# A sparse expert layer fetched in two steps: half rows, a mask, and tokens read from PSUM

## The reference, cut to what matters

```python
eidx = jnp.take_along_axis(cand_idx, pos, axis=-1)     # (token, head, 16)
g = jax.nn.softmax(best, axis=-1)
u = jnp.take(expert_u, eidx, axis=0)
h = jax.nn.gelu(jnp.einsum('thkd,td->thk', u, xb))
vv = jnp.take(expert_v, eidx, axis=0)
return jnp.einsum('thk,thkd->td', (g * h).astype(xb.dtype), vv)
```

## Time and profile before

| | before |
|---|---|
| median of 3 runs | 3214.2 us (3211.79 to 3214.63) |
| span of the profiled execution | 3210.9 us |
| PE, DVE, ACT, POOL busy, share of the span | 79%, 49%, 33%, 18% |
| DMA, mean | 333 GB/s |
| rows of the expert layer | from 1816 us to 3202 us |

### The profile page before, as it was taken

How to read it: one execution, slowest core, us unless ns; L and a number is a source line. 1 busy time by engine, 2 the same in 40 slices (tenths; PEclk the granted TensorE clock), 3 DMA queues, 4 the chain that set the end, 5 groups by cost and what they waited for, 6 DMA issues and landing times.

```text
span 3210.9 us, 43682 instructions
## 1 busy us (share of the span) xinstructions
PE 2530.9 (79%) x17242; PEld 1248.3 (39%) x17242; DVE 1564.1 (49%) x3391; ACT 1048.7 (33%) x2457; POOL 581.5 (18%) x535
## 2 busy tenths in 40 slices
PE   8999988797988878878879878897778655555655
PEld 6677774484322222222228634343324211111111
DVE  4655655763100100100107466678675777777764
ACT  2533443521000000000006354577344444343433
POOL 0000000000000000000000143344443444444442
PEclk9999998998999999999999989898888777788778
DMA  4211302249999999999995499999999999999997
GB/s 152 101 58 66 122 26 112 92 158 382 427 427 427 427 427 427 427 427 427 427 411 195 176 418 399 417 418 383 420 419 420 420 420 419 420 419 420 420 419 331
DMA packets 128670, 1067.80 MB, mean 333 GB/s; under 512 B 14289, under 2 KB 17233, under 8 KB 27601
## 3 DMA queue, kind: packets, MB, share of 16 engines
q0 software_dynamic: 75456, 543.20, 41.0%
q1 hardware_dynamic: 53008, 521.81, 39.4%
HBM read 1051.58 MB, written 13.37 MB: 332 GB/s over the span
## 4 chain that ended last, share of the span: by engine, by line
DMA 50%; PE 34%; DVE 7%; ACT 6%; issue 2%; POOL 1%; ACTq 0%; DVEq 0%; SPq 0%; POOLq 0%
PE ps L92 33%; DMA gb<-in_peer_uv,eidx 27%; DMA gw<-in_eu 14%; DMA gw<-in_ed 8%; DVE gb L146 2%; PE ps L97 2%; ACT L168 1%; ACT dots L168 1%; ACT diag L168 1%; ACT prob L168 1%; POOL gb L86 1%; DVE prob L146 0%; DVE w_lo L115 0%; ACT prob_t L168 0%; DVE prob L120 0%
## 5 line engine op out<-in xcount | busy, mean ns | idle before, releaser
L92 PE MATMUL ps<-gb,diag 64*64 64x512 f32 x4096 | 662.0, 759 | 410.3 <-ACT diag L168 396.8
L146 DVE CUSTOM_DVE_ANT_0 gb<-gb,xn 128x1024 f32<-128x1024 f32 x512 | 627.1, 1225 | 378.5 <-DMA gb<-in_peer_uv,eidx 378.0
L86 POOL DMA_INDIRECT gb<-in_peer_uv,eidx x512 | 570.3, 1114 | 1312.6 <-PE ps L92 718.5
L92 PEld LDWEIGHTS ps<-gb,diag 64*64 64x64 f32 x4096 | 148.2, 155 | 847.6 <-ACT diag L168 746.3
L168 ACT ACTIVATE dots<-dots 128x1 f32<-128x1 f32 (+1 forms) x382 | 77.6, 203 | 618.3 <-DVE dots L146 611.5
L115 DVE TENSOR_TENSOR expert_act<-expert_act,ps 128x512 f32<-128x512 f32 x32 | 22.0, 687 | 523.8 <-PE ps L92 523.2
L92 PE MATMUL ps<-ga,xt 128*64 128x512 f32 x1024 | 229.2, 596 | 41.3 <-DMA ga<-in_eu 32.6
L92 PE MATMUL ps<-gw,xt 128*64 128x512 f32 x992 | 224.3, 601 | 25.4 <-DMA gw<-in_eu 16.2
L168 ACT ACTIVATE diag<-cons,dots 128x128 f32<-128x128 f32 x512 | 205.5, 401 | 41.1 <-ACT dots L168 0.4
L115 DVE TENSOR_TENSOR x<-x,ps 128x512 f32<-128x512 f32 (+1 forms) x96 | 61.4, 643 | 296.5 <-PE ps L92 294.9
L168 ACT ACT_TABLE_LOAD x124 | 159.1, 1283 | 8.1 <-PEq L3241 0.7
(11 more groups left out here) (360 smaller groups left out, 3616.9 us busy)
## 6 DMA issues: line engine op xcount, KB each, us to landing
ga<-in_eu SPq DMA_DIRECT2D x47, 2048.0 KB, 35.5
gw<-in_eg SPq DMA_DIRECT2D x46, 2048.0 KB, 30.7
ring<-in_wt SPq DMA_DIRECT2D x75, 1024.0 KB, 6.0
gw<-in_ed SPq DMA_DIRECT2D x32, 2048.0 KB, 35.5
ga<-in_ed SPq DMA_DIRECT2D x32, 2048.0 KB, 36.1
ga<-in_eg SPq DMA_DIRECT2D x17, 2048.0 KB, 32.2
gw<-in_eu SPq DMA_DIRECT2D x16, 2048.0 KB, 35.5
p_scratch<-spill SPq DMA_DIRECT2D x35, 256.0 KB, 2.1
```

What stands on the lines that cost most here:

```text
L86: self.e.indirect_dma_start(out, None, table, bass.IndirectOffsetOnAxis(ap=idx, axis=0)).then_inc(s, 16)
L92: i = self.e.matmul(out, l, r, start=st, stop=sp, skip_group_check=True)
L146: self.done(self.e.tensor_tensor_reduce(out=o, in0=a, in1=b, scale=scale, scalar=start, op0=o0, op1=o1, accum_out=acc), name)
```

## The change

Rows 0 to 255 and 496 to 511 stay as they are. Of rows 256 to 495, each quad (four rows, n // 4) has one "whole" row, fetched as before (n % 4 == 0, but not rows 256 and 384), and three split ones. The table is seen as 32768 rows of 4 KB (`halves`), so index 2e is u and 2e + 1 is v. POOL fetches u of a split row; after the dots of the quad DVE makes the v indices and adds 65536 to those whose dot is at or below -11, which takes them past the end of the table, and POOL's second gather leaves these out. DVE also sets their weight to zero. 58 rows are whole and 182 are split; the v gathers of the first ten split rows (quads 64 to 66) fetch all, the other 172 are "gated". Of the 172 times 128 picks, 9610 fall at or below -11 by the same count as above (43.7%, 55.9 in a gather).

Four of the 13 buffers are kept for whole rows, nine are cut in a u and a v piece. A u piece is free after its dot, a v piece after its sum. The sums run one to two quads after the dots. The tokens of blocks 2 and 3 are written to PSUM (banks 0 to 3), and DVE's products read them there. The core of the diff:

```diff
+            self.e.indirect_dma_start(out, None, table, at, bounds_check=last, oob_is_err=False).then_inc(s, 16)
@@ second pass, its end @@
-        dv.wait_ge(("ffn_g", p))
+        dv.wait_ge(("ffn_g", p), ("f", p, 5))
         for i in (a, b_):
-            dv.tt(XN[i], XN[i], rowb, MUL, name=("xn3g", i))
+            dv.tt(XN[i] if i < 2 else XP[i - 2], XN[i], rowb, MUL, name=("xn3g", i))
@@ peer_order @@
+        g, j = n // 4, n % 4
+        before = [m for m in quad(g - 1) if whole(m)] if g > HALVED // 4 else []
+        later = [m for m in quad(g - 2) if not whole(m)] if g > HALVED // 4 + 1 else []
+        todo = later + before if g % 32 == 1 or g > WHOLE // 4 else before + later
+        return todo[j * len(todo) // 4:(j + 1) * len(todo) // 4]
@@ pe_peer @@
                 pe.wait_ge(("diag", n))
+                if not whole(n):
+                    pe.wait_ge(("v_row", n))
@@ ac_peer @@
+            elif ev[0] == "k":
+                ac.wait_ge(("mask", n // 4) if HALVED <= n < WHOLE else ("dot", n))
+                ac.act(d, d, ACT.Gelu_apprx_tanh, name=("gelu", n))
@@ dv_choose @@
         dv.stt(eidx[i % 2][:, 16 * h:16 * h + 16], e12[:, 0, :], 128.0, e12[:, 1, :], MUL, ADD, name=("eidx", i, h))
+        if i >= 2:
+            w_ = eidx[i % 2][:, 16 * h:16 * h + 16]
+            if (i, h) != (3, 7):
+                w_ = w_[:, 0 if h else 4:16:4]
+            dv.ts(w_, w_, 0.5, MUL, name=("eidx", i, h))
@@ dv_peer @@
-                dv.ttr(u, u, XN[i], 1.0, 0.0, MUL, ADD, dots[:, i % 2, k:k + 1], name=("dot", n), free=True)
+                dv.ttr(u, u, XN[i] if i < 2 else XP[i - 2], 1.0, 0.0, MUL, ADD, dots[:, i % 2, k:k + 1], name=("dot", n), free=True)
+            elif ev[0] == "k" and HALVED <= ev[1][0] < WHOLE:
+                if gated(n // 4):
+                    dv.ts(far, d, NO_GELU, ALU.is_le, FAR, MUL)
+                    dv.stt(e, far, 1.0, e, ADD, ADD, name=("v_idx", n // 4))
+                    dv.stt(s4, d, NO_GELU, s4, ALU.is_gt, MUL, name=("mask", n // 4))
+                else:
+                    dv.ts(e, e, 1.0, ADD, name=("v_idx", n // 4))
@@ po_peer @@
+        def v_row(n):
+            po.wait_ge(("v_idx", n // 4))
+            po.wait_ge(freed)
+            po.gather(v_of(n), halves, eidx[i % 2][:, k:k + 1], f"gv{s}", ("v_row", n), 2 * 16384 - 1 if gated(n // 4) else None)
+        for n in range(HALVED + 4):
+            u_row(n)
+        for g in range(HALVED // 4, WHOLE // 4):
+            for n in quad(g + 1):
+                u_row(n)
+            for n in quad(g):
+                if not whole(n):
+                    v_row(n)
+        for n in range(WHOLE + 4, 512):
+            u_row(n)
```

More of the change, by code:

```diff
@@ L2770, in block_program, with whole @@
     ROW_BUFFERS += [(t, GROW, ("used", 2 * TILES - 1)) for t in LATE]
[L2772 to L2777, removed]
-            held[s] = n
-        return slots
-    ROW_SLOTS = row_slots()
-    def row_group(n):
-        return (n,) if n < GROW or n >= LAST else (n, n + 1)
+    def whole(n):
+        return n < HALVED or n % 4 in (0,) and n % 128 != 0 or n >= WHOLE
@@ new lines, in quad, with places @@
+    def quad(g):
+        return range(4 * g, 4 * g + 4)
+    def places(rows, pieces, end, start=None):
+        held, out = list(start or [None] * len(pieces)), {}
+        for n in rows:
+            s = min((held[s] is not None, held[s] if held[s] is not None else s, s)
+                    for s, (_, first, _) in enumerate(pieces) if n >= first)[2]
+            freed = pieces[s][2] if held[s] is None else ("sum", held[s]) if held[s] < HALVED else (end, held[s])
+            out[n] = (s, freed, held[s] is None or held[s] < HALVED)
+            held[s] = n
+        return out, held
@@ new lines, in block_program @@
+    FIRST_AT, first_last = places(range(HALVED), ROW_BUFFERS, "sum")
+    KEEP = sorted(range(len(ROW_BUFFERS)), key=lambda s: first_last[s])[:4]
+    PAIRED = [s for s in range(len(ROW_BUFFERS)) if s not in KEEP]
+    KEPT = [(ROW_BUFFERS[s][0], 0, None) for s in KEEP]
+    U_PIECES = [(ROW_BUFFERS[s][0][:, 0:1024], 0, None) for s in PAIRED]
+    V_PIECES = [(ROW_BUFFERS[s][0][:, 1024:2048], 0, None) for s in PAIRED]
+    SPLIT = [n for n in range(512) if not whole(n)]
+    U_AT, u_last = places(SPLIT, U_PIECES, "dot", [first_last[s] for s in PAIRED])
@@ new lines, in u_of, with v_of, gated @@
+    def u_of(n):
+        return row_at(n)[0][:, 0:1024] if whole(n) else U_PIECES[U_AT[n][0]][0]
+    def v_of(n):
+        return row_at(n)[0][:, 1024:2048] if whole(n) else V_PIECES[V_AT[n][0]][0]
+    def gated(g):
+        return HALVED // 4 <= g < WHOLE // 4 and not any(V_AT[n][2] for n in quad(g) if not whole(n))
+    def row_group(n):
+        if n < GROW or n >= LAST:
+            return (n,)
+        if n < HALVED:
+            return (n - n % 2, n - n % 2 + 1)
+        return tuple(quad(n // 4))
@@ L2786, in peer_order @@
+    SUMS = [m for n in range(512) for m in sums_after(n)]
+    assert sorted(SUMS) == list(range(512)) and all(a // 128 <= b // 128 for a, b in zip(SUMS, SUMS[1:]))
+    SUM_AT = {m: q for q, m in enumerate(SUMS)}
+    ROW_ENDS = [SUMS[127], SUMS[255], SUMS[383], LAST - 1]
+    assert SUMS[LAST - 1] == LAST - 1
     def peer_order():
@@ L2791, in peer_order @@
         pass_rows = [24 + 31 * k // 10 for k in range(-1, 52)]
[L2792 to L2793 removed]
+        for n in range(512):
             group = row_group(n)
[L2795 to L2796 removed]
+            if n >= HALVED or n == group[0]:
+                ahead = 16 + min(8, n) + max(0, min(8, (n - 8) // 4))
+                need = min(32 * STEPS, STEPS * (ahead + (n if n >= HALVED else group[-1])) // 16) if n > 2 else STEPS
             while done < need:
@@ L2869, in pe_peer @@
             elif ev[0] == "w":
[L2870 to L2883, removed]
+                n = ev[1]
```

147 lines of the change are left out of this document (102 added, 45 removed).

## The result

The changed kernel took 3231.27 us (median of 4 runs, 3225.31 to 3232.83) beside 3213.64 for the kernel before (3211.79 to 3214.63): ratio 1.0052, 95% interval 1.0038 to 1.0066. It is slower by 0.5%, where 3152.6 us and a gain were forecast, and it lies outside the range. The same kernel measured in two other jobs gave 1.0087 (1.0066 to 1.0108), 3238.93 us in 4 runs, and 0.9913 (0.9884 to 0.9942), 3185.46 us in 2 runs. A job is a group of kernels that ran one after the other on one chip, with its own runs of the kernel before, which took 3213 to 3216 us in every one. Most of this document is about that difference between jobs.

What follows compares the result with a forecast made beforehand. DMA, full at 420 GB/s, was taken to bound the kernel before; after the change POOL, 533 us, plus 9 for waits and 5 for ends, 547 against 608.6, gives 3152.6 us; range 3120 to 3212.

Steps and rivals of the forecast that it cites:

- Sums one to two quads later hold v pieces longer, but nine pieces last three quads: Buffers for v halves: later sums cost nothing, as POOL asks for v(g) when sums of g - 3 are a quad old.
- the same matmuls: PE's work taken as unchanged, 1.46 us a row and 5.8 a quad, costed at nothing.
- POOL's work, 8.8 us a quad: POOL in the stretch: 422 gathers at 1.262 us a step, 533 us, 8.8 for a quad of seven.
- The bound check at zero: Comparing indices on gated gathers adds nothing on POOL; rival, chance 0.12: every tenth of a us adds 17.2 us.
- The new wait, 0.15 us a quad: POOL waiting for the v index before a quad's v gathers: 0.15 us on each of 60 quads, 9 us.
- the late-index rival: The two-quad index chain passes 17.6 us, POOL idles 0.6 us a quad: 3180 us, chance 0.18.
- the working: Index chain: v_idx(g) to the index two quads on takes 16.4 us, with 5.44 from gather start to product; slack 1.2.
- DMA: DMA in the stretch: 8.55 us a quad, 526 us in all; share 0.93 to 0.97, below POOL.
- Tokens in PSUM: Products reading PSUM stay at 1225 ns and no longer disturb POOL's gathers, taken at 0.96 us.
- The ends: Short queue at rows 496 to 511 and four whole rows costing more DMA: 5 us for both ends.
- picks not left out: Rival: an index past the end still moves data, DMA carries 624 us: 3235 us, slower, chance 0.03.

Runs made afterwards that it cites:

- e9: Kernel before with tokens of blocks 2 and 3 in PSUM and two gathers of 4 KB picks a row from row 256 on (u half twice): 3229.96 us.
- f2: The kernel before with tokens in PSUM and two 4 KB-pick gathers per row from row 256 on, repeated unchanged in another job: 3302.57 us.
- e8: Changed kernel with two rows in four split instead of three, six buffers for whole rows: 3174.78 us, ratio 0.9873.
- e5: Changed kernel with the tokens of blocks 2 and 3 back in SBUF: 3237.52 us.
- e6: Kernel before with only the tokens of blocks 2 and 3 in PSUM: 3213.68 us, ratio 1.0001.
- f4: Changed kernel a third time, unchanged, alone in another job (F): 3185.46 us, ratio 0.9913.
- e11: Changed kernel with two rows in four split and no pick left out: 3222.80 us, ratio 1.0026.
- e12: Changed kernel with one row in four split, picks left out as in the changed kernel: 3197.33 us, ratio 0.9946.
- e7: Kernel before with two gathers of 4 KB picks a row from row 256 on, both fetching the u half, tokens in SBUF: 3303.79 us.
- e1: Changed kernel with the limit at -1e30, so every gated gather fetches all 128 halves: 3228.86 us.
- e2: Changed kernel with the limit at 1e30, so every gated pick is left out: 3223.58 us.
- e10: Kernel before with each row from 256 on in two gathers of 64 picks of 8 KB (first 64 indices twice): 3480.78 us.

## Why the prediction was wrong, step by step

**The step that failed in the result.** "Sums one to two quads later hold v pieces longer, but nine pieces last three quads", and PE with "the same matmuls", both costed at nothing. That counts PE's matmuls, and not when their signals arrive; the cover it names for the v pieces is a quad, 8.8 us. Two waits hang on a sum: ACT's diagonal on the one four rows back, and POOL's v gather on the one three quads back. In late jobs signals came up to 14 us late, the circle of diagonal, matmul, signal, diagonal ran dry, and POOL waited for pieces. Beside that stands a second step, the wait for the index, set at 0.15 us a quad. In job A POOL stood idle for 65.5 us beyond the usual 0.305, in some 48.4 quads: 31 us for the index, 0.64 a quad, and 34 more for pieces, 0.71 a quad. 4 x 1.26 + 3 x 1.31 + 0.64 + 0.71 = 10.3 us a quad, against 10.15 before: the stretch is longer than before, where 547 us were forecast. Without the 0.71 it is 9.6, which is the pace of job F below. The kernel before has no late signal in its trace (job A); it issues a gather every 2.54 us and has ten queued, and its time was the same in all seven jobs.

That ACT and POOL wait for late sums, and that these waits are what the slow jobs have and the others don't, is shown by e9 and f2, and by the changed kernel in jobs A and F. Why the signals come late isn't, nor whether something else behind them sets the pace (above). What the runs show: late signals only in some jobs (five of seven), and there many of them only where gathers are dense: 40 to 56 in 100 at one gather in some 1.47 us, 74 of 228 at 1.55 (e8), 34 of 201 at 1.51 (e5), 6 of 210 at 2.54 (e6). And always together with missing records, and not PE's alone: of the 16 landings that each gather's transfer reports, the trace of f4 has 5801 for 364 gathers in the window, that of the changed kernel in job A 2002 for 339; of DVE's signals it is 722 of 727 against 270 of 679. All executions were recorded by the profiler, so whether recording takes part in it, or suffers from the same cause, stays open.

**The rest, from the job without late signals** (f4), where the steps can be judged one by one. Products of rows 255 and 499, and the stretch:

```profile
2553.50 1.23 DVE L150 CUSTOM_DVE_ANT_0 gb<-gb,xn 128x1024 f32<-128x1024 f32 x1 [0.17 <-DMA gb<-in_peer_uv,eidx]
...
3140.76 1.22 DVE L150 CUSTOM_DVE_ANT_0 gb<-gb,ps_pair 128x1024 f32<-128x1024 f32 x1 [1.28 <-DMA gb<-in_peer_uv,eidx]
```
```profile
2500.00:3100.00 600.00, 334.39 (x2040) 101.52 (x2040) 450.38 (x1232) 238.95 (x641) 402.74 (x413) 0.78 0.98 372
```
```profile
L88 POOL DMA_INDIRECT gb<-in_peer_uv,eidx x207 | 198.1, 957 | 63.1 <-issue 59.1 <-PE ps L96 2.4 <-DVE eidx L130 0.6
L90 POOL DMA_INDIRECT gb<-in_peer_uv,eidx x157 | 156.8, 999 | 82.3 <-issue 33.5 <-DVE pos L124 16.0 <-DVE soft L124 14.3
L172 ACT ACTIVATE diag<-cons,dots 128x128 f32<-128x128 f32 x208 | 83.5, 402 | 17.9 <-PE ps L96 0.4
```

587.3 us apart, 31.2 less than before, about half of the forecast's 61.6.

- *POOL's work, 8.8 us a quad*: right. 4 x (0.957 + 0.305) + 3 x (0.999 + 0.305) = 8.96, 67% busy in the earlier trace rows's window (70% forecast). POOL is the bound together with its wait, next point.
- *The bound check at zero*: 0.94 became 1.00 us, 0.06 a gather, 0.18 a quad, 10 us in all. It is far below the 0.36 at which that rival decides.
- *The new wait, 0.15 us a quad*: this step failed by its size, and the late-index rival (3180 us) is what happened in this job. POOL waited 34.4 us ahead of the first v gather beyond the usual 0.305, in 52 quads, 0.66 each; in 37 of 52 the gap was over 0.5 us. 60 x 0.66 = 40 us instead of 9. From the first v gather of a quad to the index two quads on the chain took 18.3 us in the mean of 51, where the working has 16.4 - 0.26 = 16.1. Its products and small steps are right (6.84 us, 6.9 in the working); from the whole row's gather to its product it took 7.52 us, not 5.44. That figure was read from an empty queue, and with a DMA share of 0.98 the queue isn't empty. The second miss is smaller: a gather that really waits starts 0.8 us after its release, not 0.26:

```profile
2815.48 0.94 POOL L88 DMA_INDIRECT gb<-in_peer_uv,eidx  x1 [0.30 <-issue]
2816.18 0.23 DVE L126 TENSOR_SCALAR far<-dots 128x4 f32<-128x4 f32 x1
2816.45 0.16 DVE L130 SCALAR_TENSOR_TENSOR eidx<-far,eidx 128x4 int32<-128x4 f32 x1
2817.40 1.00 POOL L90 DMA_INDIRECT gb<-in_peer_uv,eidx  x1 [0.98 <-DVE pos L124]
```

  The index is done at 2816.61, 0.19 us after POOL's gather, and the next starts at 2817.40; in all 37 it is 0.79 to 0.81. Together 18.3 + 0.8 = 19.1 us for two quads, 9.55 a quad: about the measured pace, 500/364 x 7 = 9.62.
- *DMA*: right in its terms (e8, e11, e12 above), but its share was 0.98, where 0.93 to 0.97 was forecast. A pick left out isn't quite free: packets under 512 bytes rose by 12521, which is 16 for each of 182 more gathers and 9609 more, one for each of the 9610 picks. They took 9 ns each in the median, as against 159 for a 4 KB packet.
- *Tokens in PSUM*: right. The products take 1213 ns there and 1222 in SBUF, so the extra access time that the Trainium skill gives for PSUM (Perfetto Trace Analysis, Optimizing Scalar/DVE Operations) isn't seen, and the disturbance of POOL is gone (958 and 1201 ns, changed kernel and e5).
- *The ends*: from the product of row 499 to the end it was 40.0 us and is 43.4, 3.4 more, where 5 were set for both ends.

**The range and chances.** 3120 to 3212 holds 3185 and not 3231. No rival had its place in the path from PE back to POOL, and 0.14 was left for slower, all of it on the bound check and on picks not left out. The kernel before couldn't show that path under load: its gathers are twice as far apart. That 3185 lies near the 3180 of the late-index rival is no luck, since the traces show that very wait, 0.66 us a quad for the rival's 0.6; the forecast of 3152.6 was missed by over 30 us even there. The prediction's sums come out when they are redone; only the 3.3 us around the span are 1.8 to 2.1 in every execution for which both times are known, and no term rests on them.

## What to carry to other kernels

When a change makes one engine issue more often, price the signals that come back to it too: list each wait of the new loop, the slack that it has, and whether the trace of before has ever run that path at the new rate. Split only as many transfers as the next bound needs: two rows in four give up a third of the skipped bytes, leave the issue queue slack, and were 1.3% faster than before in two jobs with late signals (C and G), while three in four lost in two such jobs (A and E). Their 3171 to 3175 us are even under the 3185 of three in four in the job without late signals. And repeat a surprising result, unchanged, in another job before explaining it: theory S was formed and seemed confirmed by e7 and e8 in late jobs, and fell as a rule for every job with one job of the other sort.

## What the runs showed of the hardware

- The same kernel, with the same time of the kernel before beside it, took 3229.96 us in one job and 3302.57 in another (e9, f2), and the changed kernel 3185 and 3231 to 3239. PE's semaphore signals were late in five jobs of seven when POOL had gathers to issue about every 1.3 us, and in those jobs no kernel got more than one gather in 1.46 us through. The medians of the kernel before agreed within 0.1% in all seven.
- An index past the bound still costs a packet of under 512 bytes, 9 ns instead of 159 in the median. On POOL a gather with a bound takes 1.00 us instead of 0.94 to 0.96, and it is the same whether no index lies past it (e1, 995 ns), some (f4, 999) or all (e2, 1005).
- A gather that POOL had to hold back for its index started 0.79 to 0.81 us after DVE had finished it (f4, 37 times).
- 4 KB picks run at 409 GB/s (e9), 8 KB picks at 420 (before).
- A gather of 64 picks of 8 KB takes POOL 0.90 us, hardly less than one of 128 (0.94). And DMA then moves 292 GB/s at a share of 1.02, with 454 ns for an 8 KB packet instead of 315. In this busy time line of e10, 138 rows are through in 500 us; why isn't known:

```profile
2600.00:3100.00 500.00, 246.56 (x1152) 59.80 (x1148) 248.63 (x588) 140.78 (x391) 247.97 (x276) 0.64 1.02 292
```
